# A joined attention, expert and recurrent-mixer kernel: one unsplit first weight piece, a layer norm shared with ScalarE, a GpSimd subtraction, and two up-projection pieces in plain float32

## The reference

```python
def first_block(x, ...):
    t = moba_attention(h, a_w_in[j], a_w_out[j], rel_bias)          # 8 heads of 128, causal, T5 bias
    h = layer_norm(DEEPNORM_ALPHA * h + t, ln_g[i, 0], ln_b[i, 0])
    f = moe_ffn(h, ...)                                             # 32 experts, top 4, SwiGLU of width 1024
    h = layer_norm(DEEPNORM_ALPHA * h + f, ln_g[i, 1], ln_b[i, 1])
    return h

def second_block(x, ...):
    h = rmsnorm(x, pre_mix_g[l])
    z = jnp.einsum('btd,dc->btc', h, w_in[l])                       # 3584 columns
    mix_a = hgrn2_mixer(q_p, f_p, i_p, g_p, lb_all[l], hgrn_norm_g[l])
    mix_b = gate_b * causal_dwconv(gate_c * conv_h, conv_w[l])
    mix = jnp.einsum('btc,cd->btd', jnp.concatenate([mix_a, mix_b], axis=-1), w_out[l])
    x = x + rmsnorm(mix, post_mix_g[l])
    h = rmsnorm(x, pre_ffn_g[l])
    u = causal_dwconv(jnp.einsum('btd,df->btf', h, ffn_w_up[l]), ffn_conv_w[l])
    gate, val = jnp.split(u, 2, axis=-1)
    y = jnp.einsum('btf,fd->btd', jax.nn.silu(gate) * val, ffn_w_down[l])   # width 2816
    return x + rmsnorm(y, post_ffn_g[l])
```

## Time and profile before

| quantity | us |
|---|---|
| median of 3 runs | 1390.52 (1390.02 to 1390.92) |
| the profiled execution's own time | 1391.46 |
| its span, first to last instruction | 1389.7 |
| TensorE busy | 1344.8 |
| VectorE, ScalarE, GpSimd busy | 448.1, 349.1, 45.1 |
| start to the last scatter of the experts | 1044.6 |
| start of the up products, and their length | 1194.3, 127.2 |

### The profile page before, as it was taken

How to read it: one execution, slowest core, us unless ns; L and a number is a source line. 1 busy time by engine, 2 the same in 40 slices (tenths; PEclk the granted TensorE clock), 3 DMA queues, 4 the chain that set the end, 5 groups by cost and what they waited for, 6 DMA issues and landing times.

```text
span 1389.7 us, 17045 instructions
## 1 busy us (share of the span) xinstructions
PE 1344.8 (97%) x7364; PEld 724.9 (52%) x7364; DVE 448.1 (32%) x740; ACT 349.1 (25%) x567; POOL 45.1 (3%) x57
## 2 busy tenths in 40 slices
PE   8999999999999999969999999999998999999997
PEld 7996333333333333313333333333336998899986
DVE  5565121112111111011111111111108776788853
ACT  5451011101101110000111011100115545666642
POOL 2000000000000000000000000000001000022200
PEclk9999999999999999979999999999999999999999
...
GB/s 375 285 242 350 421 421 429 431 430 429 431 431 430 431 431 430 431 429 431 431 430 431 430 432 431 430 430 430 430 428 208 153 152 177 127 183 183 182 121 31
DMA packets 44202, 484.17 MB, mean 348 GB/s; under 512 B 4732, under 2 KB 4784, under 8 KB 13408
## 3 DMA queue, kind: packets, MB, share of 16 engines
...
HBM read 481.99 MB, written 1.06 MB: 348 GB/s over the span
## 4 chain that ended last, share of the span: by engine, by line
PE 85%; DMA 11%; DVE 3%; issue 1%; ACT 1%; SPq 0%; DVEq 0%; ACTq 0%
PE bank L793 27%; PE bank L612 20%; PE bank L801 14%; DMA ring<-in_moe_w_gate_up 8%; PE bank L1082 4%; PE bank L813 4%; PE bank L766 3%; PE bank L594 3%; PE bank L785 2%; DMA ring<-in_w_in 2%; PE bank L1039 2%; PE bank L709 2%; PE bank L991 1%; PE bank L620 1%; DMA ring<-in_a_w_in 1%
## 5 line engine op out<-in xcount | busy, mean ns | idle before, releaser
L793 PE MATMUL bank<-ring,arena 128*64 128x512 f32 x2032 | 449.2, 599 | 9.5 <-DMA ring<-in_moe_w_gate_up 9.4
L793 PEld LDWEIGHTS bank<-ring,arena 128*64 128x64 f32 x2032 | 143.0, 138 | 314.1 <-issue 293.2
L1668 DVE TENSOR_SCALAR arena<-bank 128x512 f32<-128x512 f32 x32 | 22.1, 692 | 659.4 <-PE bank L793 659.4
L801 PE MATMUL bank<-ring,arena 128*64 128x512 f32 x1024 | 227.0, 595 | 1.8 <-DMA ring<-in_moe_w_down 1.3
L612 PE MATMUL bank<-x_hi,w_split 128*128 128x256 f32 x1152 | 214.4, 287 | 3.8 <-DVE w_split L1484 2.4
L612 PEld LDWEIGHTS bank<-x_hi,w_split 128*128 128x128 f32 x1152 | 183.7, 195 | 5.4 <-issue 4.4
L1470 DVE TENSOR_TENSOR w_split<-ring,w_split 128x2048 fp32r<-128x2048 f32 x65 | 148.6, 2290 | 85.0 <-ACT w_split L1137 85.0
L612 PE MATMUL bank<-x_lo,w_split 128*128 128x256 f32 x576 | 164.5, 286 | 0.0
L1239 ACT ACTIVATE arena<-arena 128x512 f32<-128x512 f32 x32 | 20.2, 630 | 499.6 <-DVE arena L1668 499.6
L1137 ACT CAST w_split<-ring 128x2048 fp32r<-128x2048 f32 x65 | 123.9, 1909 | 80.3 <-PE bank L612 44.9
L801 PEld LDWEIGHTS bank<-ring,arena 128*64 128x64 f32 x1024 | 70.8, 137 | 137.2 <-issue 128.1
...
## 6 DMA issues: line engine op xcount, KB each, us to landing
...
```

Of the source, the lines that this page charges most:

```text
L793: last = mm(bank[q // 2][half * 64:half * 64 + 64, :], chunk(xeT, c), w[:, c % 2, q * 512:(q + 1) * 512], start=False, stop=c == KC - 1)
L801: last = mm(bank[3][half * 64:half * 64 + 64, :], chunk(actT, c), w[:, c % 4, half * 512:(half + 1) * 512], start=c == 0, stop=c == KC - 1)
```

## The change

Five edits are joined.

1. **Start.** Piece 0 of the attention weights is no longer split: `first_product` multiplies it in plain float32, half by half as x and the piece land. Piece 1 is loaded and split in halves instead (`split_second`). The fillers ahead are three instead of five. SyncE waits for `proj_ps` as well before it loads x by token.
2. **Layer norm between the blocks.** ScalarE takes the sums of tile 1 (`tile_sums`: a copy with a sum for the mean, then squares around that mean); VectorE computes the mean from them (`mean_ready`) and no longer runs `bn_stats` on tile 1. VectorE's work is in a new order: tile 0 centred and stretched, then tile 1. ScalarE casts `IN2 + 1` and `IN2 + 2` later.
3. **GpSimd** subtracts the cast of piece `IN2` from the piece, in VectorE's place.
4. **Output projection.** The mixer's output is turned ahead of `mix(0, 1)`; tile 0 is finished ahead of `mix(1, 1)`; tile 0's `xn` is turned in the middle of `mix(1, 3)`, and its eight chunks go unsplit into a new buffer `x_full` (`take_tile`, half on ScalarE, half on VectorE). The nine fillers are gone.
5. **Up projection.** The pieces f = 2 and 3 (`DIRECT`) are not split. `direct(f, t)` multiplies them in plain float32 with `x_full`, 16 matmuls of 128 columns for each tile: tile 0 ahead of the turns of tile 1, tile 1 in the loop over f. The products use four banks by turns instead of two, and the waits that count split pieces are renumbered.

The changed lines, without the unchanged ones around them and without a few declarations:

```diff
@@ -46,7 +46,10 @@
-DOWN, PIECES = UP + FB, UP + FB + FB // 2
+DIRECT = (2, 3)
+UP_SPLIT = tuple(f for f in range(FB) if f not in DIRECT)
+DOWN = UP + FB - 2
+PIECES = DOWN + FB // 2
@@ -144,7 +147,7 @@
-summed = [D if n in (4, 5) or n >= 7 else 1 for n in range(13)]
+summed = [D if n in (3, 4, 5) or n >= 7 else 1 for n in range(13)]
@@ -259,6 +263,14 @@
+def up_bank(f):
+    return bank[4 + (f + 2) % 4]
+def up_piece(f):
+    return UP + UP_SPLIT.index(f)
@@ -446,12 +460,18 @@
-    sp.dma_start(a_place(p), a_w_in[p, :, :]).then_inc(attn_w[p % 8], 16)
+    if p == 1:
+        half = HALF // 2
+        sp.dma_start(a_place(1)[:, 0:half], a_w_in[1, :, 0:half]).then_inc(second_in, 16)
+        sp.dma_start(a_place(1)[:, half:HALF], a_w_in[1, :, half:HALF]).then_inc(attn_w[1], 16)
+    else:
+        sp.dma_start(a_place(p), a_w_in[p, :, :]).then_inc(attn_w[p % 8], 16)
+sp.wait_ge(proj_ps, 1)
@@ -511,8 +531,12 @@
+elif pos < DOWN_POS and pos - UP_POS in DIRECT:
+    sp.wait_ge(up_ps, pos - UP_POS + 1)
+elif pos < DOWN_POS:
+    sp.wait_ge(lo_ready, up_piece(pos - UP_POS) + 1)
-    sp.wait_ge(lo_ready, UP + pos - UP_POS + 1)
+    sp.wait_ge(lo_ready, DOWN + pos - DOWN_POS + 1)
@@ -565,6 +589,9 @@
+pool.wait_ge(hi_ready, IN2 + 1)
+pool.tensor_tensor(like(w_lo, IN2), pieces[IN2][2], like(w_hi, IN2).bitcast(f32), ALU.subtract
+                   ).then_inc(lo_ready, 1)
@@ -593,20 +620,19 @@
-def product(p, dst, tokens_stationary=False, fresh=0, moving=(x_hi, x_lo)):
-    pe.wait_ge(*((first_lo, 1) if p == 0 else (lo_ready, p + 1)))
+def product(p, dst, tokens_stationary=False, fresh=None, moving=(x_hi, x_lo)):
+    pe.wait_ge(lo_ready, 1 if p == 1 else p + 1)
-            if p == 0 and j == 0 and c == KC // 2:
-                pe.wait_ge(xT_lo, 2)
-                pe.wait_ge(lo_ready, 1)
-            if fresh and j == 0:
-                pe.wait_ge(hT_hi, fresh * KC - KC + c + 1)
-                pe.wait_ge(hT_lo, fresh * KC - KC + c + 1)
+            if p == 1 and j == 0 and c == KC // 2:
+                pe.wait_ge(lo_ready, 2)
+            if fresh is not None and j == 0:
+                pe.wait_ge(hT_hi, fresh + c + 1)
+                pe.wait_ge(hT_lo, fresh + c + 1)
@@ -620,9 +646,19 @@
-repeat(0, 5, zeros[:, 0:P], zeros)
-pe.wait_ge(xT_hi, 1)
-pe.wait_ge(xT_lo, 1)
+repeat(0, 3, zeros[:, 0:P], zeros)
+def first_product(dst):
+    for k, arrivals in enumerate(((xa_in, first_in), (xb_in, attn_w[0]))):
+        for arrival in arrivals:
+            pe.wait_ge(arrival, 16)
+        for j in range(2):
+            for c in range(k * KC // 2, (k + 1) * KC // 2):
+                last = mm(dst[:, j * T:(j + 1) * T], pieces[0][2][:, c, j * P:(j + 1) * P], x_feat[:, c, :],
+                          start=c == 0 and j == 0, stop=c == KC - 1, skip_group_check=True)
+    yield None
+    yield last
@@ -950,22 +989,18 @@
-def turn_tokens(src, ready, ps):
-    def half(b, j, t):
-        return turn(bank[b][:, j * T + t * P:j * T + (t + 1) * P],
-                    src[:, t, (2 * b + j) * P:(2 * b + j + 1) * P])
-    pe.wait_ge(*ready(0))
-    for b in range(4):
-        for j in range(2):
-            half(b, j, 0)
-    pe.wait_ge(*ready(1))
-    for b in range(4):
-        half(b, 0, 1)
-        half(b, 1, 1).then_inc(ps, 1)
-turn_tokens(xn, lambda t: (xn_ready, t + 1), hT_ps)
+def turn_tile(b, t):
+    for j in range(2):
+        last = turn(bank[b][:, j * T + t * P:j * T + (t + 1) * P], xn[:, t, (2 * b + j) * P:(2 * b + j + 1) * P])
+    return last
+pe.wait_ge(xn_ready, 1)
+for b in range(4):
+    turn_tile(b, 0)
+pe.wait_ge(xn_ready, 2)
+for b in range(4):
+    turn_tile(b, 1).then_inc(hT_ps, 1)
@@ -1015,7 +1050,7 @@
-for half, last in enumerate(product(IN2 + r, bank[r % 4], r >= 10, fresh=r == 0)):
+for half, last in enumerate(product(IN2 + r, bank[r % 4], r >= 10, fresh=None if r else 0)):
@@ -1026,25 +1061,37 @@
-def mix(t, k):
+def mix(t, k, chunks=range(4)):
-    for c in range(4):
+    for c in chunks:
+        if k == 2 and t == 0:
+            pe.wait_ge(mT_lo, c + 1)
+def direct(f, t):
+    place = (UP_POS + f) % W2_PLACES
+    pe.wait_ge(w2_in[place], w2_count[UP_POS + f])
+    w = w2_place(UP_POS + f).rearrange("p (c g n) -> p c g n", c=KC, g=2)
+    for g in range(2):
+        start = g * T + t * P
+        for c in range(KC):
+            last = mm(up_bank(f)[:, start:start + P], w[:, c, g, :], x_full[:, c, t * P:(t + 1) * P],
+                      start=c == 0, stop=c == KC - 1)
+    return last
-pe.wait_ge(lo_ready, OUT2 + 2)
-mix(0, 1)
@@ -1053,23 +1100,34 @@
+pe.wait_ge(lo_ready, OUT2 + 2)
+mix(0, 1)
+for g in range(2):
+    pe.wait_ge(lo_ready, OUT2 + 3 + g)
+    mix(0, 2 + g).then_inc(mix_ps, 1)
-for t in range(NT):
-    for g in range(2):
-        if t == 0:
-            pe.wait_ge(lo_ready, OUT2 + 3 + g)
-            pe.wait_ge(mT_lo, HG)
-        mix(t, 2 + g).then_inc(mix_ps, 1)
-repeat(0, 6)
-pe.wait_ge(x3_ready, 2 * NT)
-repeat(0, 3)
-turn_tokens(xn, lambda t: (xn_ready, NT + t + 1), hT_ps)
+mix(1, 2).then_inc(mix_ps, 1)
+mix(1, 3, (0, 1))
+pe.wait_ge(xn_ready, NT + 1)
+for b in range(4):
+    turn_tile(b, 0).then_inc(hT_ps, 1)
+mix(1, 3, (2, 3)).then_inc(mix_ps, 1)
+pe.wait_ge(hT_hi, KC + 4)
+pe.wait_ge(hT_lo, KC + 4)
+for f in DIRECT:
+    direct(f, 0)
+pe.wait_ge(xn_ready, NT + 2)
+for b in range(4):
+    turn_tile(b, 1).then_inc(hT_ps, 1)
-    if f >= 2:
-        pe.wait_ge(up_ready, f - 1)
-    for last in product(UP + f, bank[4 + f % 2], fresh=2 * (f == 0)):
-        pass
+    if f >= 4:
+        pe.wait_ge(up_ready, f - 3)
+    if f in DIRECT:
+        pe.wait_ge(hT_lo, 3 * KC + 4)
+        last = direct(f, 1)
+    else:
+        for last in product(up_piece(f), up_bank(f), fresh=None if f else KC + 4):
+            pass
@@ -1131,7 +1189,7 @@
-act.wait_ge(up_ps, p - UP - SPLITS + 1)
+act.wait_ge(up_ps, UP_SPLIT[p - UP - SPLITS] + 1)
@@ -1144,19 +1202,18 @@
-def split_first(j):
-    act.wait_ge(attn_w[0] if j else first_in, 16)
+def split_second(j):
+    act.wait_ge(*(pieces[1][0:2] if j else (second_in, 16)))
-    copy(like(w_hi, 0)[:, chunks, :], pieces[0][2][:, chunks, :]
-         ).then_inc(*((hi_ready, 1) if j else (first_hi, 1)))
+    copy(like(w_hi, 1)[:, chunks, :], pieces[1][2][:, chunks, :]).then_inc(hi_ready, 1)
-    split_first(j)
-split_hi(IN1 + 1)
+for j in range(2):
+    split_second(j)
@@ -1282,10 +1339,19 @@
-split_hi(IN2 + 1)
+def tile_sums(first, func, **scale):
+    for g in range(2):
+        activate(squares_at(g * 512, 512), bank[5 + 2 * g][:, :], func, accum_out=ss2[:, first + g:first + g + 1],
+                 **scale).then_inc(x_sq, 1)
+act.wait_ge(moe_done, 2)
+tile_sums(8, ACT.Copy)
+act.wait_ge(mean_ready, 1)
+tile_sums(10, ACT.Square, bias=mean[:, 0:1])
-split_hi(IN2 + 2)
@@ -1293,7 +1359,9 @@
+split_hi(IN2 + 1)
+split_hi(IN2 + 2)
@@ -1399,16 +1467,24 @@
-split_hi(UP)
-def squares_of(t, banks, ps, junk, done):
+def take_tile():
+    act.wait_ge(hT_ps, 4 + 2)
+    for c in range(KC // 2):
+        activate(x_full[:, c, 0:P], bank[c // 2][:, c % 2 * T:c % 2 * T + P], ACT.Copy,
+                 scale=vcol[:, 140 + c:141 + c]).then_inc(hT_hi, 1)
+def squares_of(t, banks, ps, junk, done, between=False):
+        if between and g:
+            take_tile()
-    squares_of(t, (4 + 2 * t, 5 + 2 * t), mix_ps, squares_at, mix_sq)
+    squares_of(t, (4 + 2 * t, 5 + 2 * t), mix_ps, squares_at, mix_sq, t == 1)
@@ -1416,7 +1492,9 @@
-evict_hi(4, 140)
+    if t == 0:
+        split_hi(UP)
+evict_hi(8, 140)
@@ -1431,17 +1509,18 @@
-split_hi(UP + f + SPLITS)
+if f not in DIRECT:
+    split_hi(up_piece(f) + SPLITS)
-    last = activate(cv[:, f % 2, g * T:(g + 1) * T], bank[4 + f % 2][:, g * T:(g + 1) * T], ACT.Copy,
+    last = activate(cv[:, f % 2, g * T:(g + 1) * T], up_bank(f)[:, g * T:(g + 1) * T], ACT.Copy,
-copy(u[:, :, 2:T + 2], bank[4 + f % 2][:, :].rearrange("p (g n) -> p g n", g=2)
+copy(u[:, :, 2:T + 2], up_bank(f)[:, :].rearrange("p (g n) -> p g n", g=2)
@@ -1477,19 +1556,19 @@
-def split_first(j):
-    dve.wait_ge(*((hi_ready, 1) if j else (first_hi, 1)))
+def split_second(j):
+    dve.wait_ge(hi_ready, j + 1)
-    tt(like(w_lo, 0)[:, chunks, :], pieces[0][2][:, chunks, :], like(w_hi, 0)[:, chunks, :].bitcast(f32),
-       ALU.subtract).then_inc(*((lo_ready, 1) if j else (first_lo, 1)))
+    tt(like(w_lo, 1)[:, chunks, :], pieces[1][2][:, chunks, :], like(w_hi, 1)[:, chunks, :].bitcast(f32),
+       ALU.subtract).then_inc(lo_ready, 1)
-    split_first(j)
-split_lo(IN1 + 1)
+for j in range(2):
+    split_second(j)
@@ -1703,41 +1782,56 @@
-split_lo(IN2)
-def sum_root(n, sums, first):
+def sum_root(n, sums, first, eps=RMS_EPS):
-    ts(variance[:, c:c + 1], sums[:, first:first + 1], sums[:, first + 1:first + 2], D * RMS_EPS, ALU.add, ALU.add
+    ts(variance[:, c:c + 1], sums[:, first:first + 1], sums[:, first + 1:first + 2], D * eps, ALU.add, ALU.add
-dve.wait_ge(ln1_in, 32)
-for t in range(NT):
-    dve.wait_ge(moe_done, t + 1)
-    for g in range(2):
```

(69 more changed lines are left out.)

15 lines of the change are left out of this document (12 added, 3 removed).

## The result

| | before | after |
|---|---|---|
| median, us | 1390.7 (1390.02 to 1390.92, 4 runs) | 1380.49 (1379.9 to 1381.5, 4 runs) |
| profiled execution's own time and span | 1391.46, 1389.7 | 1380.81, 1379.0 |

The 1390.52 that the forecast starts from is the median of the first three of these runs. The ratio is 0.9928, with a 95% interval of 0.9911 to 0.9945: 10.2 us faster, where 8.9 was forecast. On another chip the changed kernel had 1381.24 (8 runs) beside 1391.19, ratio 0.9921 (0.9890 to 0.9951). I subtract the spans, which differ by 10.7 us.

A forecast was written before the change was run, and what follows sets the result against it. Saturated DMA bounds the expert stage, released by attention steps; then TensorE's chain bounds the second block. Start -1.7, norm and clock -3.2, output and up -4.0 sum to -8.9: 1390.5 to 1381.6 us, range 1379.5 to 1384 (chance 0.66).

The forecast's parts named there:

- Start: Attention stage's first weight pieces: piece 2's product 2.5 us earlier, less 0.8 for a possible clock fall: -1.7 us.
- Order of the layer norm: Layer norm between the blocks: VectorE starts earlier and loses tile 1's statistics, so the last `xn` comes sooner: -2.0 us.
- Clock ahead of the second block: TensorE's gap before the second block's first product shrinks; clock stays up in more than half of executions: -1.2 us.
- GpSimd's subtraction: Second block's first piece, subtracted on GpSimd: ends at 1046.0 by scaling the hold, VectorE does not wait: 0 us.
- the rival: Layer norm between the blocks: GpSimd's subtraction holds VectorE's `refine(2)` until 1052.7, +5.8 us, 1387.4; chance 0.12 (1384 to 1388).
- Output and up: Mixer output, second norm and up loop: f=0 starts 0.4 us later, f=2 and f=3 save 4.4: -4.0 us.
- the case with both clocks up: TensorE's clock stays up at both gaps, the start's and the second block's: -10.6 us, 1379.9, within the forecast's range.
- rival with a loss: GpSimd holding VectorE (0.12, 1384 to 1388), front or norm gain lost (0.14, 1383 to 1387), or slower than before (0.03).
- the slower one: Layer norm: GpSimd's subtraction so long that it decides the norm; sum turns at 8.9 us of waiting; chance 0.03.

The follow-up runs named there:

- the norm kernel: Kernel before with only the layer norm between the blocks and GpSimd's subtraction changed: 1387.79 us, ratio 0.9985 (0.9976 to 0.9994).

## Why the prediction was right

- **Start, -1.7: measured -2.98, the worst of the three sums and outside its own ends (-2.5 to -0.8).** The mechanism held (piece 2's product at 22.37, set by VectorE's subtraction; forecast 22.6). Mis-sized was the clock, twice. The 0.8 us that I took off for a fall after the new gap did not come: the gap was 1.32 us, since piece 1's product ran until 21.05, later than my 20.6 (the bias table's small product had waited for its load until 14.09). And the full gain on piece 2's product was 2.85 us (25.22 to 22.37; the sum has 25.1 where the row has 25.2). I did not see that half of it is the clock of the kernel *before*, which was at 0.50 from 13.3 to 16.7. Where that fall is absent, the same product starts at 23.66 and 23.78 and the last attention products at 100.66 and 100.79: the work alone saves 1.2 to 1.4 us, the clock 1.4 to 1.6. The 2.98 itself is one pair of executions. The changed kernel profiled again has its cast at 1036.46, 3.70 earlier than before, and of the norm kernel's 1.44 only 1.02 is left at its cast.
- **Order of the layer norm, -2.0: measured -2.01,** which is partly luck. The last `xn` starts 1.82 us sooner after the cast (15.16 instead of 16.98), where 1.94 was forecast. The rest, 0.19, is the turns at full clock (0.24, less small losses), which this term did not hold. GpSimd's part of it is 0.4.
- **Clock ahead of the second block, -1.2: measured -1.81.** The granted clock stayed up in every profile that had the new norm and its fillers undisturbed (26.17 or 26.18 us for the 216 records in seven); the four with the old norm have 27.68 to 28.34. The forecast's end of -2.1 took 0.12 us for each record, 25.9; none had less than 26.17.
- **GpSimd's subtraction, 0: measured 0.** But its length was put at 3.9 us by one scaling and at 5.9 to 10.6 by the other, and it took 4.51. The second would have cost 1.1 us or more, so the 0 was a choice between them, though a fair one. An eighth of 4.51 is 0.56, less than the least (0.733) of the row that I scaled: as far as the two forms compare, part of the short one does not grow with the width. The Trainium skill ("GPSIMD Engine Reference", Elementwise — side-by-side cycle accounting) gives 4.497 us for a two-input add of 2048 float32 elements, and the trace's 4.51 for the subtraction agrees. The margin was 0.4 us: the subtraction placed later cost 4.4 us, so the rival was real and was decided by the place.
- **Output and up, -4.0: measured +0.49 and -4.39,** forecast +0.4 and -4.4. Tile 1's direct products cost 3.58 us for each of f = 2 and 3, forecast 3.56, and nothing in the loop waits for SP's later loads: 864 records in 103.67 us, 0.12 each.

The terms add to 10.70, the difference of the spans. The forecast was low by 1.8 in the span, nearly all in the start (1.3) and the clock (0.6). The median, 1380.5, is between the forecast and the case with both clocks up (1379.9), which is what happened; from 1390.52 it moved 10.0 us where the span moved 10.7, so that its error is 1.1 and not 1.8 is chance. No rival with a loss came true; the slower one is bounded now: on two-input instructions the same subtraction costs 4.4 us and 1.5 through the clock (27.69 instead of 26.18), not the 8.9 that would be needed.
